# One engine order in a two-layer hybrid decoder: TensorE's runs of one array shape in the even mixing part

## The reference, cut to what matters

```
p = rmsnorm(h, norm_w) @ w_in                      # -> rq, rk, rv, rg, sh, gb
q, k = rotary(rq), rotary(rk) * RET_DK**-0.5
o, s_ret = retention_chunked(q, k, rv, s_ret)      # o = q S + (q k^T * decay) v
xs = sh + (prev - sh) * mu                         # token shift -> r, kr, vr, wd, ad
w = -softplus(-(w0 + tanh(wd) @ w2)) - 0.5;  a = sigmoid(a0 + ad @ a2)
kk = l2norm(kr * k_k);  kr = kr * (1 + (a - 1) * k_a)
# 8 heads of 64, for each token:
s_kk = S @ kk_t
S = S * exp(log_decay_t) - s_kk (kk_t * a_t)^T + v_t k_t^T;  y_t = S @ r_t
out = concat([ret_part * silu(rg), rwkv_part * silu(gb)]) @ w_out
```

## Time and profile before

| | us |
|---|---|
| median of 3 runs | 3106.28 |
| profiled execution, its own time | 3103.8 |
| its span | 3101.8 |
| TensorE matmul busy | 2999.8 |
| VectorE busy | 1930.9 |
| ScalarE busy | 1003.0 |
| even mixing part, first matmul to last | about 721 to 1570 of the span |

### The profile page before, as it was taken

The page is one execution under the profiler, slowest core; times in us unless marked ns, Lnnn a source line. Parts: engine busy times, 40 slices in busy tenths (PEclk is TensorE's granted clock), DMA queues, the critical chain, the costliest instruction groups (busy, mean ns, idle before and its releaser), DMA issues. The chain is left out here.

```text
span 3101.8 us, 89481 instructions
## 1 busy us (share of the span) xinstructions
PE 2999.8 (97%) x38740; PEld 2724.6 (88%) x38740; DVE 1930.9 (62%) x4060; ACT 1003.0 (32%) x2220; POOL 503.7 (16%) x519
## 2 busy tenths in 40 slices
PE   9999999996999999999989999999997999999998
PEld 8999999996888887888789999999995688888886
DVE  5212344445777777777445156776765688888886
ACT  5211210003343343343167122222223344444441
POOL 0000000001333333343300000000001111111112
PEclk9999999998999999999899999999998999999999
DMA  8421221215233433433353221221214223333333
GB/s 260 120 87 60 74 75 63 67 50 175 73 109 114 121 115 106 121 120 108 108 197 115 67 71 61 77 78 60 77 50 156 77 84 99 97 100 97 96 104 130
DMA packets 227704, 311.69 MB, mean 100 GB/s; under 512 B 34793, under 2 KB 166129, under 8 KB 227185
## 3 DMA queue, kind: packets, MB, share of 16 engines
q1 hardware_dynamic: 213840, 260.30, 26.4%
q0 software_dynamic: 9152, 29.94, 3.3%
q10 hardware_dynamic: 4320, 15.73, 1.8%
HBM read 210.18 MB, written 95.72 MB: 99 GB/s over the span
## 5 line engine op out<-in xcount | busy, mean ns | idle before, releaser
L414 DVE SCALAR_TENSOR_TENSOR po_stage<-po_work,po_cw,po_stage 128x424 f32<-128x424 f32 (+1 forms) x360 | 232.1, 645 | 28.3 <-issue 1.7
L595 PE MATMUL po_ps<-po_xnT_hi,po_w_hi 128*128 128x424 f32 x960 | 205.0, 355 | 0.0
L595 PE MATMUL po_ps<-po_xnT_hi,po_w_lo 128*128 128x424 f32 x960 | 204.4, 355 | 0.0
L595 PE MATMUL po_ps<-po_xnT_lo,po_w_hi 128*128 128x424 f32 x960 | 204.1, 354 | 0.0
L299 ACT ACTIVATE po_work<-po_ps 128x424 f32<-128x424 f32 (+1 forms) x120 | 61.7, 514 | 407.9 <-PE po_ps L595 407.9
L595 PEld LDWEIGHTS po_ps<-po_xnT_hi,po_w_hi 128*128 128x128 f32 x960 | 180.2, 188 | 5.2
L595 PEld LDWEIGHTS po_ps<-po_xnT_hi,po_w_lo 128*128 128x128 f32 x960 | 180.4, 188 | 4.5
L595 PEld LDWEIGHTS po_ps<-po_xnT_lo,po_w_hi 128*128 128x128 f32 x960 | 180.2, 188 | 4.6
L595 PE MATMUL pe_ps<-pe_w_hi,pe_xnT_hi 128*128 128x256 f32 x1088 | 153.8, 284 | 5.5 <-ACT pe_xnT_hi L299 5.2
L595 PE MATMUL pe_ps<-pe_w_lo,pe_xnT_hi 128*128 128x256 f32 x1088 | 153.5, 284 | 0.0
L595 PE MATMUL pe_ps<-pe_w_hi,pe_xnT_lo 128*128 128x256 f32 x1088 | 153.3, 284 | 0.0
(11 more groups left out here) (463 smaller groups left out, 7140.4 us busy)
## 6 DMA issues: line engine op xcount, KB each, us to landing
me_ring<-scratch_w_lo SPq DMA_DIRECT2D x68, 512.0 KB, 3.9
mo_c<-scratch_ch_o SPq DMA_DIRECT2D x51, 512.0 KB, 3.7
scratch_ch_o<-po_stage SPq DMA_DIRECT2D x96, 212.0 KB, 1.9
scratch_tok_e<-pe_stage SPq DMA_DIRECT2D x136, 128.0 KB, 1.9
pe_raw<-in_w_in_e POOLq DMA_DIRECT2D x52, 256.0 KB, 4.3
me_xs<-scratch_ch_e SPq DMA_DIRECT2D x17, 768.0 KB, 6.8
po_raw<-in_w_in_o POOLq DMA_DIRECT2D x48, 256.0 KB, 4.0
scratch_ch_e<-pe_stage SPq DMA_DIRECT2D x52, 212.0 KB, 1.9
```

The costliest lines, as they stand in the source:

```text
L414: return nc.vector.scalar_tensor_tensor(out=o, in0=a, scalar=s, in1=b, op0=op0, op1=op1)
L595: last = nc.tensor.matmul(out, left.bitcast(F32R), right.bitcast(F32R), start=(i == 0 and k == 0), stop=(i == 2 and k == KD - 1))
```

## The change

TensorE's order within a step is rewritten in seven places; the instructions stay the same in kind and number, but `sums` writes another bank and the waits around it differ.

- `state_of_values(t)` moves from behind `solve(t)` to just ahead of `state_of_solved(t)`.
- `project(p, 2)` follows `project(p, 1)`; `key_side` a and b follow each other, between `level_X(n, 8)` and `level_T(n, 8)`.
- `project(p, 4)` moves ahead of `turn_q_k(n)`, behind `level_X(n, 16)`.
- `receptance_scores(n)` moves from behind `level_X(n, 16)` to behind `level_T(n, 16)`, and `sums(m)` from behind `project(p, 6)` to behind it; `project(p, 6)` and `project(p, 7)` follow each other.
- `sums(m)` writes C_ in place of D_ and waits for ScalarE's copy of C_ (`qkT_written`); `turn_sums(m)` takes over the wait for `tok_written`.
- VectorE: `mask(n, 8)` ahead of `masked_half(n, a)`, `turn_blocks(n, 8)` ahead of `masked_half(n, b)`, and `masked_scores(n)` behind `factors(m)` and `turn_blocks(n, 16)`.

In a step with all five tiles this makes 30 runs of one array shape on TensorE in place of 35.

```diff
--- before.py
+++ after.py
@@ -1261,7 +1261,7 @@
 
             def copy_sums(m):
                 await_(act, "pair_sums_ready", m)
-                A(head_sums, D_[:, 0:2 * P].rearrange("p (k c) -> p k c", k=2), ACT.Copy).then_inc(E["sums_copied"], 1)
+                A(head_sums, C_[:, 0:2 * P].rearrange("p (k c) -> p k c", k=2), ACT.Copy).then_inc(E["sums_copied"], 1)
 
             def level(n, b):
                 if level_count(n, b) is None:
@@ -1625,22 +1625,20 @@
                     split_weights(6)
                     split_weights(7)
                 if n is not None:
+                    mask(n, 8)
                     masked_half(n, "a")
-                    mask(n, 8)
-                if n is not None:
+                    turn_blocks(n, 8)
                     masked_half(n, "b")
-                    turn_blocks(n, 8)
                     mask(n, 16)
                 if n == 0:
                     dve.wait_ge(s_wl[2], 16)
-                if n is not None:
-                    masked_scores(n)
                 if m == 1:
                     dve.wait_ge(s_wl[3], 16)
                 if m is not None:
                     factors(m)
                 if n is not None:
                     turn_blocks(n, 16)
+                    masked_scores(n)
                     mask(n, 32)
                     diagonals(n)
                 if t is not None:
@@ -1892,14 +1890,15 @@
             def sums(m):
                 await_(pe, "squares_ready", m)
                 await_(pe, "bonus_in", m)
-                await_(pe, "tok_written", m)
+                await_(pe, "qkT_written", m - 1)
                 for k, src in enumerate((sq, z)):
                     for b in range(4):
-                        last_op = mm(D_[b * Q:(b + 1) * Q, k * P:(k + 1) * P], pair[:], src[:, b, :])
+                        last_op = mm(C_[b * Q:(b + 1) * Q, k * P:(k + 1) * P], pair[:], src[:, b, :])
                 last_op.then_inc(E["pair_sums_ready"], 1)
 
             def turn_sums(m):
                 await_(pe, "sums_copied", m)
+                await_(pe, "tok_written", m)
                 for k in range(2):
                     last_op = turn(D_[:, k * P:(k + 1) * P], head_sums[:, k, :])
                 last_op.then_inc(E["sums_ready"], 1)
@@ -2035,8 +2034,6 @@
                     level_T(n, 2)
                 if t is not None:
                     solve(t)
-                    if t < PT:
-                        state_of_values(t)
                 if n is not None:
                     level_X(n, 4)
                 if p is not None and not last_step:
@@ -2046,6 +2043,7 @@
                 if t is not None:
                     outputs_of_solved(t)
                     if t < PT:
+                        state_of_values(t)
                         state_of_solved(t)
                 if n == 0:
                     keep_clock(8)
@@ -2053,16 +2051,12 @@
                     level_T(n, 4)
                 if p is not None and not last_step:
                     project(p, 1)
-                elif p is None and n is not None:
-                    keep_clock(4)
-                if n is not None:
-                    key_side(n, "a")
-                    level_X(n, 8)
-                if p is not None and not last_step:
                     project(p, 2)
                 elif p is None and n is not None:
-                    keep_clock(6)
-                if n is not None:
+                    keep_clock(10)
+                if n is not None:
+                    level_X(n, 8)
+                    key_side(n, "a")
                     key_side(n, "b")
                     level_T(n, 8)
                 if p is not None and not last_step:
@@ -2074,17 +2068,23 @@
                         sample_ret_state(1, r)
                 if n is not None:
                     level_X(n, 16)
-                    receptance_scores(n)
+                if p is not None and not last_step:
+                    project(p, 4)
+                elif p is None and n is not None:
+                    keep_clock(4)
+                if n is not None:
                     turn_q_k(n)
                     if n == 0:
                         keep_clock(8)
                     level_T(n, 16)
-                if p is not None and not last_step:
-                    project(p, 4)
-                elif p is None and n is not None:
-                    keep_clock(4)
                 if t == PT:
                     sample_wk_state(0)
+                if n is not None:
+                    receptance_scores(n)
+                if m == 0:
+                    keep_clock(5)
+                if m is not None:
+                    sums(m)
                 if n is not None:
                     level_X(n, 32)
                 if p is not None and not last_step:
@@ -2097,20 +2097,13 @@
                     turn_factors(m)
                 if n is not None:
                     level_T(n, 32)
+                if t == PT:
+                    sample_wk_state(1)
                 if p is not None and not last_step:
                     project(p, 6)
-                elif p is None and n is not None:
-                    keep_clock(4)
-                if t == PT:
-                    sample_wk_state(1)
-                if m == 0:
-                    keep_clock(5)
-                if m is not None:
-                    sums(m)
-                if p is not None and not last_step:
                     project(p, 7)
                 elif p is None and n is not None:
-                    keep_clock(4)
+                    keep_clock(8)
                 if t == PT:
                     sample_wk_state(2)
                 if m is not None:
```

## The result

The changed kernel took 3127.56 us (median of four runs, 3124.72 to 3136.31), the kernel before 3103.89 us beside it (median of four); ratio 1.0081, 95% interval [1.0055, 1.0107]. It is slower by 24 us by the medians; the forecast was 3131 us. The profiled execution took 3136.31 us, the longest of the four.

The account below looks back on a forecast made before the run. The prediction took TensorE's own instructions to bound the even mixing part. Gain -15.2, stalls and pipeline ends +27.6 and clock falls +13.6 made +26.0 us on 3103.8, 3130 us; the median was put at 3131, range 3108 to 3149.

Parts of the forecast that it names:

- What bounds the part: Even mixing part: a step lasts as long as TensorE's own instructions, 44.26 us; every new wait there is paid in full.
- The stall: At `turn_factors`, TensorE waits 1.7 us per step for VectorE's `masked_scores`, bounds 1.4 to 2.0; sixteen steps, 27.2 us.
- R + 3.8: When TensorE reaches `turn_factors`, R being the start of `receptance_scores`; it was to be let in at R + 5.5.
- 2.93 + 1.29 us: VectorE's chain ahead of `turn_factors`: `factors`, a transpose and a drain take 2.93 us, then `masked_scores` 1.29 us.
- R + 1.19: When VectorE can start on the results of `receptance_scores`, whose start is R.
- The gain of a shared run: TensorE's step: each visit to an array shape costs 0.19 us; five fewer save 0.95 us per step, 15.2 us in all.
- The edits costed at nothing: Moves of masks, `state_of_values`, `key_side` b, `sums(m)` and `turn_sums`: other work covers their waits, so they cost nothing.
- The thin cover of `turn_sums`: Ahead of `turn_sums`, 3.5 us of TensorE work covers about 2.9 us of ScalarE copies, 0.6 us to spare.
- The ends of the pipeline: First two steps and sample tile: 1.7 us more stall, less 1.3 us for `mask(n, 8)` moved ahead in the first.
- The clock: Every second stall at `turn_factors` brings a stretch at 1.2 GHz: 8 x 1.7 = 13.6 us, bounds none to 27.
- Supply gaps taken up: Rival: a stalled TensorE may have its next instructions ready, giving back up to 9 us; no chance of its own.
- The sum: Whole kernel: -15.2 gain + 27.6 stalls + 13.6 clock = +26.0 us, median put at 3131 us.

Follow-up runs that it names:

- E1: The changed kernel with VectorE's `masked_scores(n)` put back ahead of `factors(m)`: 3117.96 us, ratio 1.0056 to the kernel before.
- E2: The changed kernel with TensorE's `receptance_scores(n)` back behind `level_X(n, 16)`, still 30 runs of one shape: 3089.51 us, ratio 0.9973 to the kernel before.
- E5: The kernel before with only `receptance_scores` moved behind `level_T` 16 and `masked_scores` behind `turn_blocks` 16: 3125.24 us, ratio 1.0078 to the kernel before.
- E8: The changed kernel with `receptance_scores(n)` back, tile 0's filler ahead of `sums(0)`, and `turn_q_k(n)` ahead of `project` 4: 3082.55 us, ratio 0.9949 to the kernel before.
- E6: The changed kernel with the first half of VectorE's `masked_scores` done twice, to lengthen the gap at `turn_factors`: 3148.51 us, one execution.
- E3: The changed kernel with tile 0's filler ahead of `sums(0)` in place of behind it: 3125.63 us, ratio 1.0082 to the kernel before.
- E7: The changed kernel with both halves of VectorE's `masked_scores` done twice, to lengthen the gap at `turn_factors` further: 3187.96 us, one execution.

## Why the prediction was right, and where it was not

- **What bounds the part: right.** TensorE waited for nobody, so a new wait was paid, if not quite in full (below). E1, E2 and E5 move the wait and the step follows.
- **The stall: right in place and cause, 0.2 us small.** It was put at 1.7 us a step and measured at 1.88. The sum's own steps: TensorE's way to `turn_factors` was R + 3.8, the rows give 3.81 less the gap; the rest of the chain took its 2.93 + 1.29 us; VectorE's start was R + 1.19 and is R + 1.37. That last term is the one mis-sized. R + 1.19 was the start of `masked_scores`, and in E1, where `masked_scores` comes first, it is 1.19 again; `factors` differs from it by a drain and by waiting for both halves of `receptance_scores`, and which of the two makes the 0.18 us was not separated. (The prediction had the drain, in its upper bound.) The view was wrong in one thing: the profile lists the gap as "issue", not as ended by `G2T`.
- **The gain of a shared run: right in size, 0.15 to 0.21 us against 0.19.** The sum of 0.95 us a step holds to 0.87 (45.27 - 1.88 = 43.39 against 44.26). E8, without the stall, confirms it: 44.26 - 43.40 = 0.86. The run of 128*64, for which no row stood, saves 0.16.
- **The edits costed at nothing: right but for one.** `sums(m)` and ScalarE's copy of C_ were said to overlap; with the scores moved back (E2) that cover is gone and 0.16 us shows. In the changed kernel `receptance_scores` lies between, and it does not show. The thin cover of `turn_sums` held.
- **The ends of the pipeline: wrong in size.** They were put at +0.4 us together. `sums(0)` ahead of the filler cost about 4.5 us at the start, and this was in the diff to be read: moving `sums` past `keep_clock(24)` moves the wait for GpSimd past it too. The last two steps lost 3.3 us more, and the prediction had no term for them. The guess of 1.7 us for longer stalls at the ends was near: the gaps of 2.30, 1.88 and 2.48 us are 1.5 us above three of 1.73.
- **The clock: the term was mis-sized.** Eight falls, 13.6 us, were forecast; the stalls brought two, in the steps with the longest gaps. Two falls that the kernel before had within the steps did not recur, and one came behind a gap elsewhere in a step. The error was to take two gaps of 1.30 and 1.70 us, each followed by a fall, as grounds for a fall behind every second stall. The Trainium skill's "TensorE: Matmul & The Clock Gate", section "Why this matters for your kernels", which warns only of longer gaps, was nearer for the 1.73 us gaps. For others it was not: of the 14 gaps of 1.90 to 2.67 us in E6, also shorter than what it warns of, eight were followed by a fall.
- **Supply gaps taken up: a rival that came true in part.** The prediction kept it in the range and out of the value. Four stalls were shorter by 3.1 us in all, because a gap of TensorE's own fell into the wait, and a fifth by 1.5 us, because a slow stretch did. That such gaps come from the supply of instructions, as the prediction has it, no run shows.
- **The sum: right partly by balance.** 27.6 + 13.6 - 15.2 = 26.0 was forecast and about 24 measured. The stalls came out near their term, but again by balance: the 16 gaps show 24.5 us, about 27 with the 0.15 us each that a matmul's record hides; 0.2 us more for each stall and 4.6 us taken up nearly cancel. The clock term was some 10 us too large even with both falls at stalls counted, and that stood in for the start's 4.5 us, the last two steps' 3.3 and a gain about 1 us smaller.

## What to carry to other kernels

Where one engine is busy throughout, order its blocks by what the other engine's chain needs first, and only then by array shape: five shared runs were worth 0.86 us a step, one late operand 1.88. Before a block is moved, follow what its result releases, through the other engine and back; here one block moved back to its place cost no run and turned a loss of 0.8% into a gain of 0.3% (0.5% with two more moves). A block that waits should not be moved ahead of a filler that used to run beside the wait: here that made the first mark 4.5 us late, though E3 could not show the worth of undoing it in the whole time.

## What the runs showed of the hardware

Going into and out of an array shape costs TensorE 0.15 to 0.21 us together, for 128*128, 64*128 and 128*64 alike.

Whether an idle gap brings its clock down to 1.2 GHz depends on more than its length. At `turn_factors`, none of nine gaps of 1.7 to 1.9 us in the changed kernel was followed by a fall, five of eight of about 2.66 us in E6 were, and four of seven of about 3.42 us in E7. The same gap of 2.48 us was followed in the changed kernel and not in E3. Shorter gaps were followed too: one of 1.30 us amid 32*32 work in the kernel before and one of 1.23 us within `receptance_scores` in the changed kernel; at `turn_factors` itself one of 1.04 us was, in E1, where others of 1.16 to 1.78 us were not. What decides between gaps of one length stays open.
